# An unused row of 384 bytes ahead of the first tile of a decoder-layer kernel

## What is computed

```python
ada = silu(c) @ w_ada + b_ada                     # 1024 x 6144 -> 6 vectors
h = rmsnorm(x, norm_mix_w) * (1 + sc_a) + sh_a
proj = h @ w_in                                   # 512 x 1024 @ 1024 x 9232
y_a = rmsnorm(gla(q, k, v, decay)) * silu(gg)     # chunks of 64 tokens
y_b = rmsnorm(gla(silu(hq), key, hi, f)) * silu(hg)
h_res = x + g_a * ((sigmoid(ma) * y_a + sigmoid(mb) * y_b) @ w_out)
h = rmsnorm(h_res, norm_ffn_w) * (1 + sc_f) + sh_f
u = causal_conv3(h @ w_up) + conv_b               # 1024 x 5632
out = rmsnorm(h_res + g_f * ((silu(gate) * up) @ w_down), final_norm_w)
```

## Time and profile before

| | |
|---|---|
| median of three runs | 874.01 us |
| profiled execution, first to last instruction | 872.2 us |
| TensorE busy | 857.7 us (98%) |
| VectorE, ScalarE, GpSimd busy | 607.5, 488.0, 252.5 us |
| transfers | 130.21 MB, mean 149 GB/s |

### The profile page before, as it was taken

The page is one execution under the profiler, slowest core; times in us unless marked ns, Lnnn a source line. Parts: engine busy times, 40 slices in busy tenths (PEclk is TensorE's granted clock), DMA queues, the critical chain, the costliest instruction groups (busy, mean ns, idle before and its releaser), DMA issues.

```text
span 872.2 us, 12717 instructions
## 1 busy us (share of the span) xinstructions
PE 857.7 (98%) x4688; PEld 710.6 (81%) x4688; DVE 607.5 (70%) x779; ACT 488.0 (56%) x739; POOL 252.5 (29%) x227
## 2 busy tenths in 40 slices
PE   7999999999999999999999999999999999999997
PEld 6778888887888888888887888888888888888885
DVE  3598988678867867774955466744444444599995
ACT  4576556577557657756756443633333333356574
POOL 2123779624122230330444000211111111534200
PEclk9999999999999999999999999999999999999999
DMA  9997497283644546455225931533333336599912
GB/s 336 354 320 130 118 209 103 74 237 112 174 145 131 146 124 178 116 163 162 79 74 181 157 97 49 145 96 96 96 96 96 96 96 228 112 270 206 233 36 97
DMA packets 149235, 130.21 MB, mean 149 GB/s; under 512 B 4743, under 2 KB 132065, under 8 KB 148928
## 3 DMA queue, kind: packets, MB, share of 16 engines
q1 hardware_dynamic: 136048, 110.84, 42.2%
q0 software_dynamic: 13136, 18.69, 12.7%
HBM read 125.31 MB, written 4.20 MB: 148 GB/s over the span
## 4 chain that ended last, share of the span: by engine, by line
PE 73%; ACT 2%; DVE 1%; POOL 0%; issue 0%; POOLq 0%
PE ps L2220 17%; PE ps L2222 17%; PE ps L2221 17%; PE ps L2653 4%; PE ps L2651 4%; PE ps L2652 4%; PE ps L2387 1%; PE ps L2542 1%; PE ps L2543 1%; PE ps L2546 1%; PE ps L2389 1%; PE ps L2367 1%; PE ps L2351 1%; PE ps L2354 1%; PE ps L2399 0%
## 5 line engine op out<-in xcount | busy, mean ns | idle before, releaser
L2220 PE MATMUL ps<-h_hi,w_hi 128*128 128x512 f32 (+1 forms) x568 | 223.3, 393 | 0.4 <-DVE w_lo L1852 0.4
L2222 PE MATMUL ps<-h_lo,w_hi 128*128 128x512 f32 (+1 forms) x568 | 219.5, 386 | 0.0
L2221 PE MATMUL ps<-h_hi,w_lo 128*128 128x512 f32 (+1 forms) x568 | 219.4, 386 | 0.0
L2220 PEld LDWEIGHTS ps<-h_hi,w_hi 128*128 128x128 f32 x568 | 106.7, 188 | 22.9 <-issue 1.0
L2221 PEld LDWEIGHTS ps<-h_hi,w_lo 128*128 128x128 f32 x568 | 106.7, 188 | 22.3 <-issue 1.0
L2222 PEld LDWEIGHTS ps<-h_lo,w_hi 128*128 128x128 f32 x568 | 106.7, 188 | 21.7
L983 POOL TENSOR_TENSOR prod<-conv 128x512 f32 x21 | 43.3, 2062 | 219.3 <-DVE conv L2062 219.3
L1384 ACT ACTIVATE conv<-ps,vecs 128x512 f32<-128x512 f32 x42 | 32.6, 778 | 132.3 <-PE ps L2222 123.9
L2058 DVE SCALAR_TENSOR_TENSOR conv<-ps,vecs,conv 128x511 f32<-128x511 f32 x44 | 33.0, 749 | 104.8 <-ACT conv L1384 102.5
L1852 DVE TENSOR_TENSOR w_lo<-raw,w_hi 128x1024 fp32r<-128x1024 f32 x46 | 58.1, 1275 | 56.1 <-ACT w_hi L1025 56.0
L1511 DVE TENSOR_TENSOR w_lo<-raw,w_hi 128x1024 fp32r<-128x1024 f32 x52 | 63.9, 1232 | 1.3 <-ACT w_hi L1017 1.2
(11 more groups left out here) (312 smaller groups left out, 1819.1 us busy)
## 6 DMA issues: line engine op xcount, KB each, us to landing
raw<-in_w_in_dram SPq DMA_DIRECT2D x44, 512.0 KB, 4.0
raw<-in_w_up_dram SPq DMA_DIRECT2D x44, 512.0 KB, 3.9
ada_w<-in_w_ada_dram SPq DMA_DIRECT2D x32, 512.0 KB, 4.5
ada_w<-in_w_ada_dram SPq DMA_DIRECT2D x8, 1024.0 KB, 9.3
g_blocks<-in_w_in_dram SPq DMA_DIRECT2D x24, 256.0 KB, 6.2
hres<-in_w_down_dram POOLq DMA_DIRECT2D x12, 512.0 KB, 8.8
raw<-in_w_down_dram SPq DMA_DIRECT2D x11, 512.0 KB, 5.1
raw<-in_w_out_dram SPq DMA_DIRECT2D x8, 512.0 KB, 5.6
```

The source lines that it names most:

```text
L2220: pe.matmul(dst, a_hi, b_hi, start=start and i == 0, stop=False)
L2221: pe.matmul(dst, a_lo, b_hi, start=False, stop=False)
L2222: last = pe.matmul(dst, a_hi, b_lo, start=False, stop=stop and i == n - 1)
```

## The change

One tile of 96 float32 values (384 bytes) for each partition is asked for ahead of `raw`. Nothing writes or reads it. No instruction, wait, transfer or shape is changed.

```diff
         sb = sbuf(ctx)
+        row_start = sb("row_start", [P, 96])
         raw = sb("raw", [P, RAW, KT, P])
         w_hi = sb("w_hi", [P, RING, KT, P], F32R)
```

## The result

| | before | changed |
|---|---|---|
| median of 14 runs each, same chip | 873.75 us | 875.06 us |
| lowest to highest | 872.4 to 874.05 | 874.61 to 875.8 |
| span of the profiled execution | 872.2 us | 873.5 us |

The ratio is 1.0019 with a 95% interval of 1.0012 to 1.0026. The kernel became slower, by 1.3 us of median and 1.8 us of mean (the ratio lies near that of the means): a small loss, but outside the scatter. The forecast was 874.0 us and no change. The measured time lies within its range, 872.0 to 876.0 us, but no change it was not.

A forecast was written before the change was run, and what follows sets the result against it. TensorE's matmul pace was taken to bound the kernel, some 98% of the time, besides head and tail. The sum was 872.2 + 0 + 0 + 0 us, plus 1.8 us around it: 874.0 us, range 872.0 to 876.0 us.

The forecast's parts named there:

- Loads into tiles of class 256, which go to class 128: Head loads into tiles moving from 256 to 128 past a multiple of 512: 0 us, bounds -0.15 and +0.15.
- Rival 3: Head loads or last stores pay for lost alignment: +0.35 us by the bounds, up to 877 us; chance 0.04.
- Matmul pace 0: TensorE's matmuls keep 226.7 ns, and 232.4 ns on comb: 0 us, with 0.5 us either way for restarts.
- Rival 1: Stationary tiles w and h at a multiple of 512 are slow, 232.4 ns per matmul: 889.6 us; chance 0.10.
- Rival 2: Only stationary tiles 256 past a multiple of 512 are slow, so comb and p0 speed up: 872.3 us; chance 0.07.
- Reading (b): Slow comb and p0 matmuls come from the distance between moving and stationary starts against 512; the change gives 0 us.
- (a): Slow comb and p0 matmuls come from their memory region, above 177,408; the change gives 0 us.
- (c): Slow comb and p0 matmuls come from the stationary tile's own start against 512; the change gives +15.6 or -1.7 us.
- VectorE, ScalarE and GpSimd 0: These engines' work in the middle of the kernel: 0 us, as they have slack or equal times.
- The tail 0 to +0.2: Last vector stages and stores of prod behind the last matmul: 0 us, bounds 0 and +0.2 us.
- Rival 4: Unused tile gets no space or starts are rounded, so tiles don't move: 874.0 us; chance 0.03.
- The rule on descriptors: Reads starting off a multiple of 256 bytes pay for unused bytes: about 0.1 us estimated for prod's stores, not summed.

The follow-up runs named there:

- b1: The kernel before, unchanged, profiled again, with TensorE at full clock from 9 to 14 us; profiled span 870.7 us.
- e7: Changed kernel with 128 unused bytes ahead of the head's tiles, back at a multiple of 256, later tiles staying; ratio to the kernel before 1.0004.
- e2: Kernel before with 384 unused bytes ahead of xT, so head tiles and comb move while raw, w and h stay; ratio to the kernel before 1.0008.
- e4: Changed kernel with the unused row at 128 bytes in place of 384; ratio to the kernel before 1.0018.
- e1: Changed kernel with a second unused row of 128 bytes ahead of xT, head tiles and comb back at 256; ratio to the kernel before 0.9990.
- e10: Kernel before with 128 unused bytes ahead of raw and 384 behind causal, every tile at a multiple of 256; ratio to the kernel before 0.9983.
- e11: Kernel before with 64 unused bytes ahead of raw and 448 behind causal, w and comb 64 apart; one run, profiled span 871.0 us.
- e5: Changed kernel with the unused row at 64 bytes in place of 384; ratio to the kernel before 1.0027.

## Why the prediction was wrong

**The failed step is the term "Loads into tiles of class 256, which go to class 128", taken as 0 with bounds of 0.15 us.** Its mechanism and its price were both in the text, as Rival 3: "a tenth on the 30 saturated us of the head would be 3 us". The rate fell by a tenth, and the last packet of the head's last `ada_w` load starts at 38.67 us where b1 has 35.95, 2.7 us later. That rival had 0.04, because "the equal rates in rows 9 speak against it". That the time still fell within the range is luck in part: the upper end allowed for a head 1.5 us slower, the loads lost 2.7, and not all of that reached the end. A second, smaller part of the step is `g_blocks`: the prediction counted this term in the head alone, since the other engines and the transfers "in the middle have slack"; at 128 us that slack was 0.3 us in b1, and the later load took it and 0.7 us more in e7.

**Why rows 9 misled.** They compared a long stretch into class 256 with 1.2 us into class 128, and the slower rate doesn't set in at once. It could be read in the kernel before, in the six loads to `raw` (class 128) that follow the head's. Busy time by stretch of the kernel before, at their beginning and at their end:

```profile
37.30:38.60 1.30, 1.30 (x8) 1.08 (x7) 1.30 (x3) 0.50 (x1) 0.00 (x0) 1.00 1.09 384
39.90:41.20 1.30, 1.30 (x38) 0.95 (x40) 0.53 (x1) 0.36 (x1) 0.00 (x0) 1.00 1.11 351
```

The transfer records say the same by packet: the first 640 of these 1536 packets take 46.0 ns each, the last 768 50.4 to 51.3. So a load off a multiple of 256 goes on at the full rate for some 640 packets (1.7 us; in b1 768) if what ran ahead of it was aligned, then falls. The two loads of rows 9 are 512 packets. e2 shows it at that very place. Its `raw` lies as before, only what is loaded ahead of it is off its multiple:

```profile
87.60:88.90 1.30, 1.30 (x7) 1.07 (x7) 1.30 (x2) 0.00 (x0) 1.16 (x2) 1.00 1.09 378
90.40:91.70 1.30, 1.30 (x7) 1.10 (x6) 1.30 (x4) 1.30 (x3) 0.00 (x0) 1.00 1.11 351
```

The second line is the pair of `raw` loads: 351 GB/s, 384 in the earlier trace rows. The converse holds too. In the changed kernel `raw` is at class 0 and its six loads come behind misaligned ones; the first 128 packets take 48.5 ns each, the next 46.2 and the next four times 128 46.0. What makes the rate lag so was not found.

**From 2.7 us of loads to 1.3 us of time.** TensorE starts the 64 matmuls on `ada_w` 2.15 us behind the start of the load's last packet when it waits for it (40.82 less 38.67). With the packet at 35.95, b1 could have started at 38.10; it started at 38.64, so it had 0.54 us in hand:

```profile
38.64 1.95 PE L2245 MATMUL ps<-ada_w,c_rep 128*32 128x128 f32 x64
```

2.72 less 0.54 is 2.18 us, and 40.82 less 38.64 is 2.18. Against the profile with the reduced clock the same sum is smaller, since there TensorE was late by itself: 40.25 less (35.78 + 2.15) is 2.32 us in hand, and the changed kernel lost 2.89 less 2.32, 0.57 us, at this place. The wait for `stash` at 131 us adds some 0.5 us in both comparisons: TensorE is then 2.6 us behind b1 and 1.0 behind the first profile. At the end of the span it is 2.8 us against b1 and 1.3 against the first profile. So the slow head and the reduced clock don't add. The one hides the other: e4 has both,

```profile
12.00:14.00 2.00, 2.00 (x31) 1.62 (x23) 0.00 (x0) 1.17 (x4) 0.00 (x0) 0.50 1.01 406
```

and ends 0.3 us behind the changed kernel, not 1.4. The runs of the changed kernel have a median span of 873.35 us. That is 2.7 us above the runs of before at the full clock (some 870.6) and 1.1 above those at the reduced one (some 872.2). Eight of the 14 runs of before that it is compared with are of the second kind (873.64 us and more), so their median falls there, and the difference of the medians is 1.3 us.

**Point by point.**
- *Matmul pace 0*: right. 226.7, 232.4 ns, no change, and Rival 1 (+15.6 us) and Rival 2 (-1.7 us) did not happen. e4 adds that `w` and `h` at class 256 keep their pace too.
- *Reading (b), the distance of moving and stationary start*: the prediction left it open among three. e1, e2, e10 and e11 show it; in them the region of `comb` is the same, and `comb` at 256 is slow in the kernel before and fast in e10, so (a) and (c) are out. Under it a shift of all tiles alike changes nothing, which is why this step held. The argument that settled it for 0, that a better aligned tile can't be the slow one, was not what decides. The Trainium skill (SBUF — State Buffer, Who interferes with whom) has two independent read ports for TensorE. By that alone the distance would not matter; the paces, 226.7 to 233.4 ns by distance alone, disagree, and the measurement decides.
- *VectorE, ScalarE and GpSimd 0*: right for the instructions themselves, whose busy time is at most 0.9 us in 608 off. The wait of TensorE for VectorE at 131 us comes from the load ahead of it, not from VectorE's pace.
- *The tail 0 to +0.2*: right, +0.1 us between the two profiles.
- *Rival 4, the change does nothing*: refuted by the head.
- *The rule on descriptors*: the prediction draws on it for the head. The Trainium skill (DMA: Bandwidth & Descriptors, How a descriptor splits into AXI transactions) speaks of reads that don't start on a multiple of 256 bytes. The prediction took its silence on writes, together with rows 9, for agreement. The runs show that writes pay: 348 GB/s in place of 386. By its count of beats a start 64 bytes off would cost half of one 128 bytes off, an estimate; e5 and the change have the same 348 GB/s, so the size of the cost is not that count's.
- *The two stalls of the head*: the text puts both down to loads; the earlier trace rows give the second to "issue".
- *The base*: the sum was made on one execution, and the kernel has two clocks in its head, 1.4 us apart; the two medians differ by 1.3.

## What to carry to other kernels

Start every tile that a saturated load fills at a multiple of 256 bytes, and the two operands of a matmul at the same place against 256; here the first is worth a tenth of the load rate, the second 5.7 ns in 232. When a price is bounded by a second stretch of the trace, take one as long as the one that is asked about, and look whether the rate holds from its beginning to its end. Where the head has a stall, work out how much each engine has in hand there before a slower load is called hidden, and do so on more than one execution. The same holds for every later place where a load leads to a wait of the engine that sets the time: here one such place had 0.3 us in hand.

## What the runs showed of the hardware that was not expected

- Loads of 1-KB rows from DRAM at saturation (18 to 28 us): 385 to 387 GB/s into tiles at 0 or 256 past a multiple of 512 (378 in e10), 348 or 349 at 128, 320 or 384, by the same share of busy transfer engines (1.09 to 1.10); 46 ns for a packet against some 51.
- The slower rate comes some 640 to 770 packets late behind aligned loads, and in the changed kernel the faster one is back after 128 to 256 packets.
- 512-column float32 matmuls take 226.7 to 226.9 ns with the two operands 0 or 256 apart against 512, 232.45 with 128 and 233.4 with 64 (one profile).
- One program, unchanged, has TensorE at 2.4 GHz from 9 to 14 us in some executions and partly at 1.2 GHz in others, with the same 15 matmuls between 5 and 9 us in both. What tips it was not found.
